# Bank choice, tile splits ahead of their use, and the order of the first loads in a two-block kernel

## The reference, cut to what matters

```
for layer in range(2):                                   # first block
    mod, mod_c = silu(c) @ w_mod + b_mod, silu(c_ctx) @ w_mod + b_mod
    h = modulate(rms_norm(x, norm_mix), shift1, scale1)
    q, k, v, hy, g = split(h @ w_in)                     # heads normed, q and k rotated
    attn = attention(q, [k_ctx, k], [v_ctx, v])
    hyo  = hyena_mix(hy, conv, filter)                   # long convolution by Fourier transform
    x = x + gate1 * (merge(attn, hyo, g) @ w_out)
    h = modulate(rms_norm(x, norm_ffn), shift2, scale2)
    x = x + gate2 * ((silu(h @ w_gate) * (h @ w_up)) @ w_down)
x = rms_norm(x, norm_final)                              # second block
u = rms_norm(x) @ w_in_2                                 # conv input, q, k, v
x = x + concat(conformer_conv(u), dilated_attention(rotary(q), rotary(k), v)) @ w_out_2
x = x + cross_attention(rms_norm(x), rms_norm(mem), w_xq, w_xk, w_xv) @ w_xo
x = x + moe(rms_norm(x), 32 experts, top 2)              # all experts' weights are read
out = rms_norm(x)
```

## Time and profile before

| | |
|---|---|
| median of 3 runs | 2172.09 us (2167.09 to 2172.17) |
| profiled execution | 2171.04 us, its span 2169.1 us |
| TensorE matmul, weight load | 1924.5 us (89%), 1560.7 us (72%) |
| VectorE, ScalarE, GpSimd | 1132.4 us (52%), 890.7 us (41%), 17.7 us (1%) |
| mean granted TensorE clock | 0.947 |
| HBM read | 424.68 MB |

### The profile page before, as it was taken

One profiled execution on the slowest core, in us unless ns is written; L12 is line 12 of the kernel. 1 busy time (PEld: TensorE's weight loads), 2 busy tenths in 40 slices (PEclk: granted clock), 3 DMA queues, 4 the chain that ended last, 5 costly groups with the idle time before them and its releaser, 6 DMA issues.

```text
span 2169.1 us, 33404 instructions
## 1 busy us (share of the span) xinstructions
PE 1924.5 (89%) x14008; PEld 1560.7 (72%) x14008; DVE 1132.4 (52%) x1862; ACT 890.7 (41%) x1514; POOL 17.7 (1%) x31
## 2 busy tenths in 40 slices
PE   5999989998999999999999999898799777777676
PEld 3877667776777877788699999897598644544444
DVE  3354756675887778557655666678565201110111
ACT  4332445564765667444444555543654200000001
POOL 1000000000000000000000000000000000000000
PEclk8999999998999999999999999999899989888987
DMA  7222014452555554224045455453145999999995
GB/s 300 82 75 78 1 63 142 150 205 80 186 176 182 190 178 157 98 88 146 1 166 204 163 180 177 153 165 108 49 147 219 420 420 420 420 417 420 421 419 229
DMA packets 90976, 427.99 MB, mean 197 GB/s; under 512 B 11073, under 2 KB 12610, under 8 KB 65858
## 3 DMA queue, kind: packets, MB, share of 16 engines
q1 hardware_dynamic: 78722, 381.13, 46.7%
q10 hardware_dynamic: 12096, 44.64, 6.2%
HBM read 424.68 MB, written 1.05 MB: 196 GB/s over the span
## 4 chain that ended last, share of the span: by engine, by line
PE 62%; DMA 19%; DVE 9%; ACT 6%; issue 3%; SPq 0%; POOL 0%; ACTq 0%; DVEq 0%; POOLq 0%
PE bank L462 40%; DMA area<-in_w 7%; PE bank L1580 7%; DMA ring<-in_w 4%; DMA HH<-in_w 4%; PE bank L477 2%; PE bank L2409 2%; PE bank L2453 2%; ACT his_r L433 1%; DVE st L1260 1%; DVE ring_r L441 1%; DMA PPT<-in_w 1%; DMA his<-in_w 1%; PE bank L1188 1%; PE bank L2061 1%
## 5 line engine op out<-in xcount | busy, mean ns | idle before, releaser
L441 DVE TENSOR_TENSOR ring_r<-ring,his_r 128x1024 fp32r<-128x1024 f32 x306 | 373.8, 1224 | 294.8 <-ACT his_r L433 293.4
L462 PE MATMUL bank<-HH_r,his_r 128*128 128x256 f32 (+1 forms) x1504 | 503.4, 335 | 3.7 <-DVE ring_r L441 2.7
L462 PE MATMUL bank<-HH_r,ring_r 128*128 128x256 f32 (+1 forms) x1504 | 492.3, 327 | 0.0
L433 ACT ACTIVATE his_r<-ring 128x1024 fp32r<-128x1024 f32 x306 | 323.3, 1059 | 392.8 <-PE bank L462 234.8
L462 PE MATMUL bank<-H_r,his_r 128*128 128x256 f32 (+1 forms) x1440 | 472.5, 328 | 0.0
L462 PEld LDWEIGHTS bank<-HH_r,his_r 128*128 128x128 f32 x1504 | 283.7, 189 | 39.8 <-issue 10.6
L462 PEld LDWEIGHTS bank<-HH_r,ring_r 128*128 128x128 f32 x1504 | 283.6, 189 | 24.3
L462 PEld LDWEIGHTS bank<-H_r,his_r 128*128 128x128 f32 x1440 | 270.3, 188 | 29.1 <-issue 2.6
L2425 DVE TENSOR_TENSOR tmp<-tmp,bank 128x128 f32<-128x128 f32 x64 | 18.4, 288 | 385.7 <-ACT tmp L2418 258.0
L1580 PE MATMUL bank<-VT_r,his_r 128*128 128x512 f32 (+1 forms) x352 | 121.8, 346 | 10.2 <-DVE YF_r L1332 9.9
L2409 PE MATMUL bank<-area,KF 128*32 128x128 f32 x1888 | 90.7, 317 | 38.1 <-DMA area<-in_w 34.2
(11 more groups left out here) (408 smaller groups left out, 3321.2 us busy)
## 6 DMA issues: line engine op xcount, KB each, us to landing
area<-in_w SPq DMA_DIRECT2D x91, 1024.0 KB, 27.0
ring<-in_w_in SPq DMA_DIRECT2D x102, 512.0 KB, 3.5
ring<-in_w_gate_up SPq DMA_DIRECT2D x88, 512.0 KB, 3.5
ring<-in_w SPq DMA_DIRECT2D x36, 1024.0 KB, 27.3
HH<-in_w SPq DMA_DIRECT2D x26, 1024.0 KB, 26.9
ring<-in_w_down SPq DMA_DIRECT2D x44, 512.0 KB, 3.4
KX<-in_w_mod_rows ACTq DMA_DIRECT2D x28, 512.0 KB, 3.4
VX<-in_w_mod_rows ACTq DMA_DIRECT2D x28, 512.0 KB, 3.5
```

Source lines behind the costliest of these rows:

```text
L433: ac.eng.activation(hi_slot(n), stream.slot(u), ACT.Copy).then_inc(*ac_hi.up(n))
L441: ve.eng.tensor_tensor(lo_slot(u), stream.slot(u), hi_slot(n).bitcast(F32), ALU.subtract).then_inc(*ve_lo.up(n))
L462: ins = pe.eng.matmul(out, a, b, start=k == 0 and m == 0, stop=end)
```

## The change

It makes seven edits. (1) `take` moves the first idle bank to the end of the list and hands it out, so the bank idle longest is used. (2) `down_cuts` gives tile 22 x half + k + 3 at step k; tiles 0, 1, 2 are cut beside tiles 12, 14 and 20 of gate_up (`CUT_BESIDE`). ScalarE waits for the product of the tile itself instead of the last one. (3) At the start, modulation group 1 moves ahead of the sums on TensorE; ScalarE copies group 0's rows ahead of the squares and group 1's behind them; the w_in splits move ahead of the rows of group 3 (ScalarE) and ahead of the modulation bias (VectorE). SP loads X behind four modulation units and the ring's first two units ahead of the last four. (4) `con` is laid out anew and loaded in two pieces: 130 columns at the start by ScalarE, the rest by SP behind ring unit 2, with a signal `dft` of its own for which the rotation and the filter spectrum wait. (5) The split of w_xk_2's second unit is called ahead of the last low part of down's end, behind square 6 on ScalarE. (6) The rotation of head 11 goes behind the first pair of value tiles. (7) In `ve_beside`, VectorE's splits of w_xv_2 belong to the step before.

```diff
         def take(self, freed_by, *key):
-        self.n += 1
-        return self.use(self.idle[self.n % len(self.idle)], freed_by, key)
+        self.idle.append(self.idle.pop(0))
+        return self.use(self.idle[-1], freed_by, key)
...
@@ ac_gate_up
+                if j in CUT_BESIDE:
+                    m = CUT_BESIDE[j]
+                    ac.wait_ge(*ve_out.at("aff", l, m))
+                    ac_cut_tile(ac, cut_place(VTR, m, t), AFF[:, m, 0:t], ("ff", l, m))
@@ ve_gate_up
+                if j in CUT_BESIDE:
+                    m = CUT_BESIDE[j]
+                    ve_cut_tile(ve, cut_place(VTR, m, t), cut_place(YFR, m, t), AFF[:, m, 0:t], ("ff", l, m))
...
         def down_cuts(half, k):
-            if k == 21:
-                return [] if half else [22, 23]
-            return [] if half and k == 0 else [0, 1] if half + k == 0 else [22 * half + k + 1]
+            m = 22 * half + k + 3
+            return [m] if m < 44 else []
+        CUT_BESIDE = {12: 0, 14: 1, 20: 2}
@@ ac_down
-            ac.wait_ge(*ve_out.at("aff", l, 21))
             for half in range(2):
                 for k in range(22):
                     for m in down_cuts(half, k):
+                        if half == 0:
+                            ac.wait_ge(*ve_out.at("aff", l, min(m, 21)))
                         if m >= 4:
                             ac.wait_ge(*pe_products.at("down", l, *divmod(m - 4, 22)))
...
                 ac_sqrt_table(ac, j, 8)
+                if l and j == 6:
+                    ac_split(ac, where["w_xk_2", 0, 1])
@@ ve_down
                 if l and half:
+                    ve_split(ve, where["w_xk_2", 0, 1])
                     ve.wait_ge(*ve_out.at("ff", l, 7, 0))
                     low(7)
@@ pe_mixer (ve_mixer alike, with taps 11 and 12 behind the split at u == 16)
-            for i in range(13):
-                if i < 12:
+            for i in range(12):
...
                 if i:
+                    pe_rotate(pe, i - 1)
             for j in range(3):
...
+                if j == 0:
+                    pe_rotate(pe, 11)
+
+        def pe_rotate(pe, i):
+            out = banks.take((ve_rope, ("sin2", i)), "rope2", i)
+            pe.wait_ge(*banks.emptied("rope2", i))
+            pe.wait_ge(*landed["late"])
+            pe.wait_ge(*ve_out.at("head2", i))
+            pe.eng.matmul(out[:, 0:N], LATE[:, 1, :], head2(i), start=True, stop=True).then_inc(*pe_rope.up("two", i))
@@ ve_beside
-            for n in value_steps(h):
+            for n in value_steps(h - 1) if h else ():
                 ve_split(ve, two_on(value_unit(n)))
@@ tensor_program
             pe_mod_group(pe, 0)
+            pe_mod_group(pe, 1)
             pe_open(pe, "mix0")
...
             pe_spread(pe, "mix0", 512)
-            pe_mod_group(pe, 1)
             pe_mod_group(pe, 2)
@@ scalar_program
-            ac.eng.dma_start(con[:, :], T["con"]).then_inc(*landed["con"])
+            ac.eng.dma_start(con[:, 0:NCON0], T["con"][:, 0:NCON0]).then_inc(*landed["con"])
...
+            ac_mod_group(ac, 0)
             ac.wait_ge(*landed["x"])
             for k in range(8):
                 ac_square(ac, "mix0", k, X[:, k, :], 512)
-                if k == 3:
-                    ac_mod_group(ac, 0)
+            ac_mod_group(ac, 1)
             ac_sqrt_table(ac, 5, 8)
             ac_sqrt(ac, "mix0", 8, 512, 1024)
-            ac_mod_group(ac, 1)
             ac_mod_group(ac, 2)
+            ac_split(ac, where["w_in", 0, 1])
             ac_mod_group(ac, 3)
-            ac_split(ac, where["w_in", 0, 1])
@@ vector_program
+            ve_split(ve, where["w_in", 0, 1])
             ve_mod_groups(ve)
-            ve_split(ve, where["w_in", 0, 1])
@@ sync_program
-            sp.eng.dma_start(X[:, :, :], T["x"]).then_inc(*landed["x"])
             for i, (name, l, u) in enumerate(first.units):
+                if i == 4:
+                    sp.eng.dma_start(X[:, :, :], T["x"]).then_inc(*landed["x"])
+                if i == 12:
+                    weights(0)
+                    weights(1)
                 sp.eng.dma_start(first.slot(i), T[name][l, u]).then_inc(first.arrived(i)[0], 16)
-            for i, (name, l, u) in enumerate(stream.units):
+            weights(2)
+            sp.eng.dma_start(con[:, NCON0:NCON], T["con"][:, NCON0:NCON]).then_inc(*landed["dft"])
+            for i in range(3, len(stream.units)):
```

More of the change, by code:

```diff
@@ L109, in shape_constants @@
         if p % 32 < 2:
-            con[p, 2816 + p % 32] = 1.0
+            con[p, CON["sel"] + p % 32] = 1.0
     fil = np.zeros((P, NFIL), np.float32)
@@ L156, in restart @@
     def restart(self):
-        self.idle, self.n, self.frees = list(range(len(self.aps))), 0, [None] * len(self.aps)
+        self.idle, self.frees = list(range(len(self.aps))), [None] * len(self.aps)
     def use(self, i, freed_by, key):
@@ L1782, in pe_mixer @@
                 pe_block(pe, ("glu", j), banks.ap("glu", j)[:, 0:N], "w_in_2", 0, 8 * j, 8, H2P, cut)
-            for i in range(13):
-                if i < 12:
-                    out = banks.take((ve_out, ("head2", i)), "head2", i)
-                    pe.wait_ge(*banks.emptied("head2", i))
-                    pe_block(pe, ("head2", i), out[:, 0:N], "w_in_2", 0, 8 * (4 + i), 8, H2P, cut)
-                if i:
-                    out = banks.take((ve_rope, ("sin2", i - 1)), "rope2", i - 1)
-                    pe.wait_ge(*banks.emptied("rope2", i - 1))
-                    pe.wait_ge(*landed["late"])
-                    pe.wait_ge(*ve_out.at("head2", i - 1))
-                    pe.eng.matmul(out[:, 0:N], LATE[:, 1, :], head2(i - 1), start=True, stop=True).then_inc(*pe_rope.up("two", i - 1))
+            for i in range(12):
+                out = banks.take((ve_out, ("head2", i)), "head2", i)
+                pe.wait_ge(*banks.emptied("head2", i))
+                pe_block(pe, ("head2", i), out[:, 0:N], "w_in_2", 0, 8 * (4 + i), 8, H2P, cut)
+                if i:
+                    pe_rotate(pe, i - 1)
             for j in range(3):
@@ L2813, in sync_program @@
                     sp.wait_ge(*signal.at(*step))
-                src = T[name][l, u] if name in T["deep"] else T[name][u]
-                sp.eng.dma_start(stream.slot(i), src).then_inc(stream.arrived(i)[0], 16)
+                weights(i)
             for i, (name, e, u) in enumerate(experts.units):
```

61 lines of the change are left out of this document (35 added, 26 removed).

## The result

| | before | after |
|---|---|---|
| first comparison, median | 2172.09 us | 2115.31 us (2110.34 to 2120.43, 4 runs) |
| ratio, 95% interval | | 0.9746 (0.9713 to 0.9779) |
| second comparison, median | 2169.25 us | 2116.39 us (2113.70 to 2120.44, 5 runs) |
| ratio, 95% interval | | 0.9760 (0.9747 to 0.9774) |
| span of the profiled execution | 2169.1 us | 2113.3 us, and again 2113.3 us |

The change makes the kernel 53 to 57 us faster by the medians, 52 to 55 by the ratios. I forecast 35 and gave 2124 us as the lower end.

A forecast was written before the change was run, and what follows sets the result against it. Data bounds the start and the expert weights the last 476 us, TensorE the middle; 4.0 + 15 + 2.0 + 2.8 + 11 = 34.8 us off 2172.1 gives about 2137, own range 2131 to 2143, wider range 2124 to 2153.

The forecast's parts named there:

- rival 5: At the end: the expert stream does not hang on the ring and no gain arrives, 2172 us; chance 0.03.
- So elsewhere I take 0: Bank rule outside dilated attention: with constant numbers of idle banks both rules give the same order, so no gain.
- Less what TensorE holds (65 us over 15 steps is 4.3 a step): Dilated attention: deduction from six times 2.4 (14.5 us); splits and banks together priced at 11, bounds 4 and 15.
- The sign that I gave: Dilated attention after the change: VectorE's masks 4.7 us apart.
- I take 15 and leave 3 to that half: Down, both layers: gain 15 us, 3 kept back for layer 1's second half; bounds 9.9 and 18.2.
- The sum of the four items: Down: 6.9 and 7.2 us lost against gate_up's rate, plus entry waits of 2.4 and 1.7, 18.2 in all.
- Keys 2.0 and rotation 2.8: Behind down: first key tiles gain 2.0 us (bounds 0 and 4), head 11's rotation 2.8 (bounds 1 and 4.7).
- Rival 2: Down, keys and group 3 at the start: the clock stays where it is, 2141 us; chance 0.13.
- Start, 4.0: Kernel start up to the first w_in tile: gain 4.0 us, between 2.5 and 5.4; first w_in tile at 40.
- Number 3: More than priced: start 5.4, down 18.2, keys 4, rotation 4.7, attention 15, giving 2125 us; chance 0.07.
- Number 1: Dilated attention: the loop through both engines does not open, gain 4 instead of 11, 2144 us; chance 0.14.
- number 4: Down: each of 44 weight units stalls behind ScalarE's cut; 0.8 us a unit cancels everything, 1.0 gives 2181; chance 0.03.

The follow-up runs named there:

- b_beside: The kernel before with only VectorE's splits of w_xv_2 moved to the step before; 2156.47 us, ratio 0.9936.
- a_nokey: The changed kernel with the split of w_xk's second unit back in its old place; 2117.60 us.
- b_down: The kernel before with only down's tiles cut ahead (tile k + 3 at step k, three inside gate_up); 2148.97 us, ratio 0.9902.
- b_bank_beside: The kernel before with only the new bank rule and VectorE's later splits of w_xv_2; 2142.46 us, ratio 0.9880.
- a_sumbank: The changed kernel with the bank of ffn0's sum given by hand to the up product of gate_up's first tile in layer 0; 2124.07 us, ratio 0.9784.
- a_nobank: The changed kernel with the old bank rule; 2126.34 us, ratio 0.9802.

## Why the prediction was wrong

**The bound and the path** were right. The expert stream is bound by its loads and starts behind the ring, and 56.7 and 52.2 us of earlier start gave 55.8 us at the end in the two profiles, within the 5 us by which that last stretch varies; rival 5 is out.

**"So elsewhere I take 0"** is the step that failed outright, worth 5.2 us. The argument was that with constant numbers of idle banks both rules give the same order. True, but the number is not constant right behind a norm: the spread gives the sum's bank back, the count can land on it at once, and VectorE reads it until the eighth tile. I had named the very condition ("a bank taken last but emptied late") and did not look for a place that meets it. The row that shows it was in TensorE's timeline, the longest idle stretch of the kernel between its start and the experts. The waits view has it too, as `PE bank L477 <- issue: 8.9, 1, 8.9`, but with no engine named as the one to blame, and I priced only waits with a name.

**"Less what TensorE holds (65 us over 15 steps is 4.3 a step)"** is the step that mis-sized attention, by 6 us. Six times 2.4, 14.5 us, was near the splits' price: alone they gave 14.8. That is in part luck: in `b_beside` seven of the eleven gaps between masks shrank by 0.8 to 4.0 us and two grew, one of them that of head 2 by 1.1 (forecast 1.2), 12.6 together, and 2.2 more came behind the last mask. I took it back to 11, banks included, with a floor made of TensorE's busy time at a clock of 0.89. At 0.95 to 1.00 the same instructions take 58 to 60 us, and the stage is 4 to 6 us longer than that. The sign that I gave, masks 4.7 us apart, came out at 4.8 beside a gain of 17 us: I had divided the stage by 15 steps, while the masks themselves stood 6.0 apart before. The banks gave 2.2 to 5.4 there, 3.0 by themselves (lower bound 4).

**"I take 15 and leave 3 to that half"** was 2.8 us too careful. The rates of the earlier trace rows were the right measure: both layers reach them, 0.229 and 0.119 us a matmul, and both entry waits are gone. The sum of the four items was 18.2, the measurement 17.8. The waits that are named would have given 10 here. The Trainium skill (Perfetto Trace Analysis, Identifying the Most-Contended Engine) says that TensorE's busy share does not tell how close it is to its limit; the trace agrees: down of layer 1 had TensorE busy for 65.5 of 69.4 us, and the stage became 6.9 us shorter.

**Keys 2.0 and rotation 2.8** were too high rather than too low. Undone together they cost 1.3 us in the median and 2.6 in the profile, against 4.8. The clock was to rise with the wait's removal; it still falls there in most profiles. What the wait itself gives back at the keys is 0.65 to 0.8 us. The Trainium skill (TensorE: Matmul & The Clock Gate, What's actually happening) has the throttled clock as the default, which activity releases. The trace agrees in so far as the clock falls behind the sums without the wait as well; the 1.3 us that I had set beside it for the key term, a single edit's median cannot tell from 2.0 (`a_nokey` is 1.2 and 2.3 us above the two medians of the changed kernel). Rival 2 was half right: the clock stayed low at the keys, but in down and in attention it rose with the holes filled.

**Start, 4.0**: 4.5 to 4.8 in the profile. The last turns ended at 36.07 (34.12 + 1.95), 0.6 later than worked out, and the idle time behind it shrank from 4.45 to 3.09 us, as the w_in splits (2.35 us on VectorE) no longer stand ahead of the norm; I had put these at next to nothing.

**Rivals.** Number 3, more than priced, was the right kind at 2125 us, and even its sum of upper bounds missed the banks at ffn0 and had attention too low by 2. Number 1 (the loop does not open) and number 4 (down stalls behind ScalarE's cut) have nothing in the profiles for them.

**The sum** with what was measured: 4.8 for the start, 5.2 at ffn0, 17.8 in down, 17.2 in attention, 2.6 for keys and rotation, together 47.6 us of the 53 that the larger of the two comparisons gives. The profiles show a further 3.3 behind down, where the profiled execution of before took longer than that of any other kernel (103.3 us against 100.1 with both edits undone, the clock at 0.50 for 6 us behind the sums and for 4 us behind the rotation's wait), and 1.5 between the first w_in tile and the context's scores, where the sixteen profiles lie between 166.1 and 168.5 us whatever the kernel. With these the sum is the 52 us of the second profile. Whether the changed kernel gains there in every execution or only in the profiled pair, and so 5 of its 53 us, stays open; the medians of `b_down` and `b_bank_beside` too fell 5 us more than their stages.

## What to carry to other kernels

A hole in the bound engine that ends in "issue" is a wait that the profile can't name: look up which buffer the next instruction takes and who read it last, above all behind a place where a buffer is given back. A busy time read at a reduced clock is no floor: scale it by the clock before it caps a gain. A profiled span is no measure of a small edit: cut it into stretches, and see which of them differ between two profiles of one program. And price a stage against the rate that the same instructions reach elsewhere in the same profile; that gave down to 0.4 us, where caution took 3 off.

## What the runs showed of the hardware

The clock behind the same instructions differs between two executions of one program: 1.00 in one profile and 0.50, then 0.79, in the other, 1.5 us of difference in that stretch. Behind one and the same wait, of 2.62 us (the rotation) or 2.2 us (the sums in attention), it stayed at 1.00 in some profiles and stood at 0.50 to 0.70 in others, which cost about 3 us in the second case. A stage whose holes are filled gets its own work cheaper: attention's matmuls took 67.7 us of busy time at a clock of 0.87 and 58.5 at 1.00. The expert stream, bound by its loads, took 507.3 to 512.3 us in sixteen profiles, 511.9 and 507.5 with one program. A stall of 5.2 us can cost 8 to 9 (`a_sumbank`) or 5 (in `a_nobank`, at the same place), by what it makes the engines behind it meet.
